# Two layers' first tiles multiplied before their norm, the last norm on turned rows, and another dealing of modulation work over the first block

## The reference

```
def second_block(x, c, ...):
    for l in range(DEPTH_2):
        x = decoder_layer(x, c, ...)
    return rms_norm_2(x, final_norm_g)

def decoder_layer(x, c, ...):
    mod = jax.nn.silu(c.astype(F32)) @ w_ada + b_ada
    shift1, scale1, gate1, shift2, scale2, gate2 = jnp.split(mod, 6, axis=-1)
    h = modulate(rms_norm_2(x, norm1_g), shift1, scale1)
    p = h @ w_in
    ...
    x = x + (gate1[:, None, :] * (merged.astype(x.dtype) @ w_o)).astype(x.dtype)
    h2 = modulate(rms_norm_2(x, norm2_g), shift2, scale2)
    y_moe = hier_moe(h2, ...)
    x = x + (gate2[:, None, :] * y_moe).astype(x.dtype)

def rms_norm_2(x, g):
    y = xf * lax.rsqrt(jnp.mean(xf * xf, axis=-1, keepdims=True) + NORM_EPS)
    return (y * g.astype(F32)).astype(x.dtype)
def modulate(h, shift, scale):
    return (h.astype(F32) * (1.0 + scale[:, None, :]) + shift[:, None, :]).astype(h.dtype)
```

## Time and profile before

| | us |
|---|---|
| median of 3 runs | 1968.52 (1965.6 to 1969.34) |
| profiled execution, its own time | 1964.88 |
| span of the profiled execution | 1963.1 |
| barrier between first block and layer 0 | 314.85 |

### The profile page before, as it was taken

How to read it: one execution, slowest core, us unless ns; L and a number is a source line. 1 busy time by engine, 2 the same in 40 slices (tenths; PEclk the granted TensorE clock), 3 DMA queues, 4 the chain that set the end, 5 groups by cost and what they waited for, 6 DMA issues and landing times.

```text
span 1963.1 us, 24328 instructions
## 1 busy us (share of the span) xinstructions
PE 1630.3 (83%) x10843; PEld 1104.7 (56%) x10843; DVE 531.9 (27%) x1049; ACT 318.3 (16%) x630; POOL 17.5 (1%) x25
## 2 busy tenths in 40 slices
PE   7999899999999996665666599999999866665666
PEld 6776678887888852222222177878888322221223
DVE  4887972644111120000000037131022100000002
ACT  2432312322200020000000042221011100000001
POOL 0010000000000000000000000000000000000000
PEclk9999899999999998878888899999999988787888
DMA  7798954313359379999999952134773999999996
GB/s 274 268 392 328 346 214 161 130 45 104 133 202 388 137 317 429 431 433 427 434 429 431 422 195 87 45 129 172 285 293 150 406 429 434 428 431 433 429 429 284
DMA packets 90364, 585.72 MB, mean 298 GB/s; under 512 B 12248, under 2 KB 15120, under 8 KB 69648
## 3 DMA queue, kind: packets, MB, share of 16 engines
q1 hardware_dynamic: 87664, 580.30, 72.8%
q10 hardware_dynamic: 2592, 3.81, 0.6%
HBM read 583.01 MB, written 1.08 MB: 298 GB/s over the span
## 4 chain that ended last, share of the span: by engine, by line
PE 47%; DMA 33%; DVE 3%; ACT 1%; issue 0%; SPq 0%
DMA expert_halves<-in_w_exp_down 18%; PE ps L1335 13%; DMA expert_halves<-in_w_exp_up 11%; PE ps L2215 8%; PE ps L2576 8%; DMA expert_halves<-in_w_exp_gate 4%; PE ps L2228 4%; PE ps L2253 3%; PE ps L2596 1%; PE ps L1338 1%; PE ps L2562 1%; PE ps L1585 1%; PE ps L1832 0%; DVE base_products L2000 0%; DVE gram L1955 0%; PE ps L1842 0%
## 5 line engine op out<-in xcount | busy, mean ns | idle before, releaser
L2576 PE MATMUL ps<-expert_halves,gathered 128*32 128x512 f32 x2048 | 308.0, 759 | 201.1 <-DMA expert_halves<-in_w_exp_up 125.2
L2576 PEld LDWEIGHTS ps<-expert_halves,gathered 128*32 128x32 f32 x2048 | 74.9, 134 | 424.3 <-issue 193.2
L1335 PE MATMUL ps<-h,ring 128*128 128x256 f32 x1216 | 274.4, 382 | 0.0
L1335 PEld LDWEIGHTS ps<-h,ring 128*128 128x128 f32 x1216 | 227.8, 190 | 37.0 <-issue 4.5
L2712 DVE TENSOR_TENSOR gate_up_rows<-gate_up_rows,ps 128x512 f32<-128x512 f32 x16 | 11.0, 688 | 735.9 <-PE ps L2576 735.9
L2576 PE MATMUL ps<-expert_halves,gate_up_turned 128*32 128x512 f32 x1024 | 144.4, 715 | 78.4 <-DMA expert_halves<-in_w_exp_down 70.5
L2215 PE MATMUL ps<-h,ring 128*128 128x256 f32 x768 | 166.7, 379 | 0.0
L2215 PEld LDWEIGHTS ps<-h,ring 128*128 128x128 f32 x768 | 145.9, 190 | 19.8
L268 PE MATMUL ps<-u,ring 128*128 128x256 f32 x640 | 146.3, 383 | 0.8 <-ACT xbc_raw L358 0.8
L2576 PEld LDWEIGHTS ps<-expert_halves,gate_up_turned 128*32 128x32 f32 x1024 | 34.9, 128 | 175.4 <-issue 84.2
L268 PEld LDWEIGHTS ps<-u,ring 128*128 128x128 f32 x640 | 119.5, 190 | 22.1 <-issue 4.2
(11 more groups left out here) (472 smaller groups left out, 1455.1 us busy)
## 6 DMA issues: line engine op xcount, KB each, us to landing
expert_halves<-in_w_exp_gate SPq DMA_DIRECT2D x30, 4096.0 KB, 43.1
expert_halves<-in_w_exp_up SPq DMA_DIRECT2D x30, 4096.0 KB, 43.1
expert_halves<-in_w_exp_down SPq DMA_DIRECT2D x26, 4096.0 KB, 43.3
ring<-in_w_in SPq DMA_DIRECT2D x31, 2048.0 KB, 9.0
ada_ring<-in_w_ada SPq DMA_DIRECT2D x48, 1024.0 KB, 7.3
ring<-in_w_gate SPq DMA_DIRECT2D x12, 2048.0 KB, 7.9
expert_halves<-in_w_exp_down SPq DMA_DIRECT2D x8, 2048.0 KB, 9.5
ring<-in_w_branch SPq DMA_DIRECT2D x6, 2048.0 KB, 7.6
```

The lines of the kernel that those rows point to most:

```text
L1335: ins = nc.tensor.matmul(k.ps[:, IN_BANK[t], 0:S], slab[:, j, c:c + w], k.h[:, j, :], start=j == 0, stop=j == ND - 1)
L2576: ins = nc.tensor.matmul(k.ps[r, bank, :], left[:, at + j, r], rows[:, i, :], start=at + j == 0, stop=last and j == 3)
```

## The change

**Dealing.** `ADA_BEHIND`, `ADA_AT`, the late places and the arguments of `scale` change. Pieces 0 to 2 stand behind slab 2 instead of slab 3 and wait for tile 0 instead of tile 7; six rows are done ahead of the last convolution, four before the scan loop (as before), one instead of two in each of its turns, up to 48 instead of 42 before the attention, and fewer in most of the attention's turns. **Early tiles.** In both layers the first two input tiles are multiplied with x times its gain (`gains`), with the shift as a 257th column; VectorE multiplies them by 1/rms afterwards and adds the shift column. The mean takes five matmuls instead of eight, since VectorE sums the first four squared tiles. Two slabs of layer 0 are asked for before the barrier, and one activation table is loaded before it. **End.** The sum over features is taken on turned rows, so that x is turned unscaled, as it becomes ready.

```diff
-ADA_BEHIND = (0, 0, 0, 3, 0, 3, 6, 5, 4, 5, 5, 5, 5, 5, 2)
+ADA_BEHIND = (0, 0, 3, 0, 0, 3, 2, 4, 7, 5, 4, 6, 4, 4, 6)
...
-ADA_AT = (19, 21, 23, 26, 30, 33, 36, 39, 41)
+ADA_AT = (18, 21, 23, 26, 29, 32, 36, 39, 41)
 ADA_STEPS = {t: [("sum", g)] for g, t in enumerate(ADA_AT)}
 ADA_STEPS |= {t + 1: [("turn", g)] for g, t in enumerate(ADA_AT)}
-LATE_STEPS = [[], [], [("sum", 9)], [("turn", 9)]] + 8 * [[]] + [[("sum", 10)], [("turn", 10)]] + 4 * [[]] + [[("sum", 11)], [("turn", 11)]] + 4 * [[]]
+LATE_AT = ((5, 6), (16, 19), (22, 23))
+LATE_STEPS = [[] for _ in range(3 * ND)]
+for _g, (_s, _t) in enumerate(LATE_AT):
+    LATE_STEPS[_s], LATE_STEPS[_t] = [("sum", len(ADA_AT) + _g)], [("turn", len(ADA_AT) + _g)]
 ada_steps = lambda t: ADA_STEPS[t] if t in ADA_STEPS else []
...
                 if p == 0:
-                    sp.wait_ge(sem.tile_done, 8)
+                    sp.wait_ge(sem.tile_done, 1)
...
+        for i in range(N_EARLY):
+            sp.wait_ge(sem.out_used, i + 2)
+            mix_load(k, sp, 0, i)
...
+        f.scale(dve, 6)
...
-        f.scale(dve, 4)
+        f.scale(dve, 10)
...
-            f.scale(dve, 4 + 2 * (r + 1))
+            f.scale(dve, 10 + r + 1)
...
-        f.scale(dve, 34)
+        f.scale(dve, 32)
...
-QK_AT = 42
+QK_AT = 48
...
-            f.scale(dve, 52 + (j + 1) * 5)
+            f.scale(dve, (56, 60, 64, 68, 76, 80)[j])
...
+        nc.scalar.preload_act_table_set("natural_log_exp_and_others")
...
-        f.scale(dve, 86)
+        f.scale(dve, 84)
...
-        f.scale(dve, 91)
+        f.scale(dve, 88)
...
+N_EARLY = 2
...
+            if t < N_EARLY:
+                if t == 0:
+                    pe.wait_ge(self.sem.gx_ready, self.past.gx_ready + j + 1)
+                ins = nc.tensor.matmul(k.ps[:, IN_BANK[t], 0:S + 1], slab[:, j, c:c + w], k.gx[:, j, 0:S + 1],
+                                       start=j == 0, stop=j == ND - 1)
+                if j == ND - 1:
+                    ins.then_inc(self.sem.tile_done, 1)
+                self.made += 1
+                continue
...
+        y.products(pe, 4)
         mean_of_squares(k, y, pe)
+        y.products(pe, N_EARLY * ND)
         if y.l == 0:
             router_products(k, y, pe)
-        else:
-            keep_busy(k, pe, 1, 9)
...
+            gains(k, y, dve, range(ND))
+            sum_four(k, y, dve)
             router_weights(k, y, dve)
+        else:
+            gains(k, y, dve, range(4, ND))
...
+        for t in range(N_EARLY):
+            dve.wait_ge(sem.tile_done, past.tile_done + t + 1)
+            nc.vector.tensor_tensor(k.early[:, t, :], k.ps[:, IN_BANK[t], 0:S], k.rstd[:, :], ALU.mult)
+            nc.vector.tensor_copy(k.early_shift[:, t:t + 1], k.ps[:, IN_BANK[t], S:S + 1]).then_inc(sem.normed, 1)
+            dve.wait_ge(sem.normed, past.normed + 2 * t + 3)
+            nc.vector.tensor_scalar(k.early[:, t, :], k.early[:, t, :], k.early_shift[:, t:t + 1], None, ALU.add
+                                    ).then_inc(sem.normed, 1)
...
+def sum_four(k, y, dve):
+
+
+    sem, past = y.sem, y.past
+    two = lambda a: k.h[:, a:a + 2, :]
+    dve.wait_ge(sem.squared, past.squared + 2)
+    dve.tensor_tensor(two(0), two(0), two(2), ALU.add).then_inc(sem.normed, 1)
+    dve.wait_ge(sem.normed, past.normed + 1)
+    dve.tensor_tensor(k.h[:, 0, :], k.h[:, 0, :], k.h[:, 1, :], ALU.add).then_inc(sem.normed, 1)
+
+
+def gains(k, y, dve, tiles):
+
+
+    mod = k.mod[:, y.l, :]
+    for j in tiles:
+        if j == 0:
+            dve.tensor_copy(k.gx[:, :, S], mod[:, 0:ND])
+        dve.tensor_scalar(k.gx[:, j, 0:S], k.x[:, j, :], mod[:, ND + j:ND + j + 1], None, ALU.mult).then_inc(y.sem.gx_ready, 1)
 
 
 def mean_of_squares(k, y, pe):
     sem, past = y.sem, y.past
-    for j in range(ND):
-        if j % 2 == 0:
-            pe.wait_ge(sem.squared, past.squared + j // 2 + 1)
-        ins = pe.matmul(k.ps[:, 2, 0:S], k.const("mean_d"), k.h[:, j, :], start=j == 0, stop=j == ND - 1)
+    pe.wait_ge(sem.normed, past.normed + 2)
+    for n, j in enumerate((0, 4, 5, 6, 7)):
+        if n % 2 == 1:
+            pe.wait_ge(sem.squared, past.squared + 3 + n // 2)
+        ins = pe.matmul(k.ps[:, 2, 0:S], k.const("mean_d"), k.h[:, j, :], start=n == 0, stop=n == 4)
...
+            if j == 3 and y.l < LAYERS - 1:
+                dve.wait_ge(sem.x_updated, past.x_updated + 4)
+                gains(k, y.next, dve, range(4))
+                sum_four(k, y.next, dve)
...
+            last = q == N_QUAD - 1 and l == LAYERS - 1
+            if last:
+                final_spread(k, y, pe)
...
+                if l == LAYERS - 1:
+                    for pair in range(2):
+                        final_turns(k, y, pe, pair)
...
+            if q == N_QUAD - 1 and y.l < LAYERS - 1:
+                for i in range(2):
+                    act.wait_ge(sem.x_updated, past.x_updated + 2 * i + 2)
+                    square_pair(k, y.next, act, i)
...
+def final_turns(k, y, pe, pair):
+
+    pe.wait_ge(y.sem.x_updated, y.past.x_updated + 2 * pair + 2)
+    for j in (2 * pair, 2 * pair + 1):
+        for t in range(NT):
+            ins = pe.transpose(k.ps[:, 2 + j // 4 * 2 + t, j % 4 * P:(j % 4 + 1) * P], k.x[:, j, t * P:(t + 1) * P], k.const("ident"))
+    ins.then_inc(y.sem.final_turned, 1)
...
+        for n, (b, t) in enumerate(((0, 0), (0, 1), (1, 0), (1, 1))):
+            act.wait_ge(sem.final_turned, 2 * b + 2)
+            if n == 3:
+                act.wait_ge(sem.final_scaled, 3)
+            nc.scalar.activation(k.final_junk[:, b, t, :], turned(b, t), ACT.Square, accum_out=k.final_sums[:, t, b:b + 1]
+                                 ).then_inc(sem.squared, 1)
+        act.wait_ge(sem.mean_done, past.mean_done + 2)
+        nc.scalar.activation(k.final_rstd[:, :], k.final_rstd[:, :], ACT.Ln, bias=k.eps[:, 0:1], scale=1.0 / D).then_inc(sem.ln_done, 1)
+        act.wait_ge(sem.ln_done, past.ln_done + 3)
+        nc.scalar.activation(k.final_rstd[:, :], k.final_rstd[:, :], ACT.Exp, scale=-0.5).then_inc(sem.rstd_done, 1)
...
+        for n, (b, t) in enumerate(((0, 0), (0, 1), (1, 1), (1, 0))):
+            dve.wait_ge(sem.final_turned, 2 * b + 2)
+            if n != 2:
+                dve.wait_ge(sem.squared, past.squared + ND // 2 + min(n, 2) + 1)
+            nc.vector.tensor_tensor(k.y_tok[:, t, cols(b)], turned(b, t), k.final_gain[:, cols(b)], ALU.mult
+                                    ).then_inc(sem.final_scaled, 1)
+        dve.wait_ge(sem.squared, past.squared + ND // 2 + 4)
+        nc.vector.tensor_reduce(k.final_rstd[:, :], k.final_sums[:, :, :], AX.X, ALU.add).then_inc(sem.mean_done, 1)
+        dve.wait_ge(sem.rstd_done, past.rstd_done + 3)
```

More of the change, by code:

```diff
@@ L1196, in first_block @@
     first_memory(k)
+    k.mix_loaded = [nc.alloc_semaphore(name=f"mix_slot{i}_loaded") for i in range(SLOTS)]
     one = [nc.alloc_semaphore(name=n) for n in FIRST_SIGNALS]
@@ L1443, in early @@
                 load_steps(3, 0, 2, sem.half_loaded[3][l])
-        for i in range(SLOTS):
+        for i in range(0 if l else N_EARLY, SLOTS):
             if l:
@@ L1595, in rwkv_inputs @@
     pair_ps = lambda b, j: k.ps[:, b + j // 2, j % 2 * S:j % 2 * S + S]
+    tile = lambda t: k.early[:, t, :] if t < N_EARLY else k.ps[:, IN_BANK[t], 0:S]
     flat = lambda t: t.rearrange("p j s -> p (j s)")
@@ L2836, in second_block @@
     memory_map(k)
-    k.mix_loaded = [nc.alloc_semaphore(name=f"mix_slot{i}_loaded") for i in range(SLOTS)]
     sems = Signals(*(nc.alloc_semaphore(name=n) for n in SIGNALS),
@@ L2845, in second_block @@
                     for l in range(LAYERS)])
+    layers = [Layer(k, l, sems) for l in range(LAYERS)]
+    for y, following in zip(layers, layers[1:]):
+        y.next = following
     with nc.Block() as block:
         for l in range(LAYERS):
-            y = Layer(k, l, sems)
+            y = layers[l]
             layer_loads(k, y, block)
@@ L2858, in second_block, with final_spread @@
             add_experts(k, y, block)
-        finish(k, Layer(k, LAYERS, sems), block)
+        finish(k, y, block)
+def final_spread(k, y, pe):
+    gain = k.cols_2[0]["final"]
+    for j in range(ND):
+        ins = pe.matmul(k.ps[:, 2 + j // 4, j % 4 * P:(j % 4 + 1) * P], gain[:, j:j + 1].broadcast_to([P, P]), k.const("ident"),
+                        start=True, stop=True)
+    ins.then_inc(y.sem.final_gain, 1)
+def final_turns(k, y, pe, pair):
[4 more added lines that the diff above has]
+    ins.then_inc(y.sem.final_turned, 1)
```

83 lines of the change are left out of this document (43 added, 40 removed).

## The result

The changed kernel takes 2018.1 us (median of 4 runs, 2014.1 to 2020.9), the kernel before 1968.9 in the same comparison: ratio 1.025, 95% interval 1.0236 to 1.0264. It is 49 us slower; the forecast was 32 slower, and the time lies 4 us above the upper end of the range. The profiled execution is the one of 2020.93 us.

A forecast was written before the change was run, and what follows sets the result against it. Bound: TensorE paces the first block; VectorE's rows wait for pieces behind slabs that wait for tiles. Sum: 36.6 + 7 - 2 - 5 - 4 = +32.6 on 1964.9, 1997.5, stated as 2000 by the median; range 1979 to 2014.

The forecast's parts named there:

- step 6: Attention: the two wide tiles cover most of the wait for pieces behind slab 10; 34.8 us behind at the output products.
- step 8: TensorE's low clock behind five new waits of 6 to 12 us: 1.4 us lost at each, 7 in all.
- steps 2 to 5: Scan loop to first logits: rows wait for pieces behind slabs that wait for TensorE's tiles; 34.6 us behind at the logits.
- step 1: Start of the scan loop: piece 3 lands at about 81.5; 2.9 us later, or 9.5 if SP is no earlier.
- (2): Third scan turn: row 12's piece stands behind slab 6; the fourth scan product starts at 104.9, 6.5 us after TensorE is ready.
- (3): Seventh scan turn: row 16's piece stands behind slab 7; the last scan product starts at 129.9, 15.9 us behind.
- (4): Sum behind tile 26: rows 24 to 31 need pieces behind slab 8 and end at 168.9; 25.1 us behind.
- (5): Sum behind tile 29 waits 9.3 us for rows 38 and 39; first logits at 205.4, 34.6 us behind.
- Step 7: Output: rows 84 to 95 stand behind slab 14, the last sum waits some 7 us; barrier at 351.4, 36.6 behind.
- Rival (b): Worse case: SP isn't earlier at the start (+6.5), low clock costs 3 us a wait (+8): 2005 to 2020, 17 in 100.
- The boundaries: Early tiles and the end: gains of 2 us in layer 0, 5 in layer 1 and 4 at the end.

The follow-up runs named there:

- the one-line kernel: The changed kernel with only the pieces put back behind their old slabs (`ADA_BEHIND`): 1962.3 us, ratio 0.9971 to the kernel before.
- e3: The changed kernel with idle matmuls on TensorE in front of six of its long waits: 2016.4 us, ratio 1.024 to the kernel before.
- e10: The changed kernel with one piece, number 8, moved from behind slab 7 to behind slab 6: 2011.5 us, ratio 1.0219 to the kernel before.
- e7: The changed kernel with ScalarE's copy of sum 10 put ahead of its square root: 2019.4 us, ratio 1.0262 to the kernel before.

## Why the prediction was right in kind and wrong in size

The time lies above the stated range, and the barrier, forecast between 348 and 365, stands at 377.50. Two steps failed: step 6 left out a wait for ScalarE, and step 8 booked too little for TensorE's low clock, at which steps 2 to 5 had not been walked. Each step's forecast beside what the trace after shows, with the miss that was added since the line above:

| place | forecast | after | miss added |
|---|---|---|---|
| first scan product (step 1: 86.82 + 2.9) | 89.7 | 92.72 | 3.0 |
| fourth scan product (2) | 104.9 | 110.38 | 2.5 |
| last scan product (3) | 129.9 | 137.88 | 2.5 |
| sum behind tile 26 (4) | 168.9 | 179.30 | 2.4 |
| sum behind tile 29 (5) | 189.8 | 202.35 | 2.2 |
| first logits (5) | 205.4 | 220.67 | 2.7 |
| output products (6: 246.75 + 34.8) | 281.6 | 307.05 | 10.2 |
| barrier (7: 314.9 + 36.6) | 351.5 | 377.50 | 0.5 |

*The mechanism was right.* All four stalls of steps 2 to 5 are where they were said to be, with waits of 6.1, 12.2, 11.7 and 9.4 for VectorE's rows (forecast 6.5, about 12, 11.4 and 9.3). That they come from the pieces behind the slabs is shown by the one-line kernel, and that they hang on each other by the one with piece 8.

*Step 6 failed*: "the two wide tiles (7.1 us each) cover most of it", "34.8 behind at the output products". The first wide tile covers 7 us, the second none if a turn stands between them that has to wait. The change moved sum 5 from tile 33 to 32, and with it the turn to tile 33, ahead of the second wide tile; that was in the table, and I walked only VectorE's rows through the attention, not ScalarE's list. ScalarE's copy of the sum stood there behind exponentials that waited for rows 48 to 51, and TensorE waited 9.5 for the copy. It is the largest single miss: 10.2 on the way to the output products, of which the kernel that moves the sum back recovers 7.9 (9.0 in the time). The place alone does no harm: the one-line kernel has its turn there too, with pieces 24 and 25 a slab earlier, and no turn of it waits over 2 us.

*Steps 2 to 5 walked TensorE at the full clock, and step 8 booked too little for it.* They missed 12.3 in sum. The stretches that TensorE runs right behind a wait, up to the slab's request or the logits, hold 11.8 of that. SP asks for slabs 8 and 9 in the change at:

```profile
158.53 0.38 SPq L390 DMA_DIRECT2D ring<-in_w_in  x1
...
189.53 0.38 SPq L390 DMA_DIRECT2D ring<-in_w_in  x1
```

| stretch of TensorE | forecast | after | with idle matmuls (e3) |
|---|---|---|---|
| first scan product to slab 6 | 2.0 | 4.0 | 2.2 |
| fourth scan product to slab 7 | 12.8 | 15.4 | 14.8 |
| last scan product to slab 8 | 18.3 | 20.7 | 19.8 |
| sum behind tile 26 to slab 9 | 8.1 | 10.2 | 8.2 |
| sum behind tile 29 to first logits | 15.6 | 18.3 | 15.9 |

In the first, fourth and fifth the idle matmuls kept the clock up, and there they come within 0.3 of the forecast. In the second and third the clock was low again even with them; but where the last scan product had hardly waited (e10), the next sum followed it in 4.2 us, against 6.5 in the change, so 2.2 of the third stretch's 2.4 are clock as well. For the second it is not shown how much is clock and how much TensorE's work that the walk left out. What lies between these stretches, slab, piece, rows, came out as walked: from slab 7 to the last scan product 12.1 (forecast 12.2), from slab 8 to its sum 20.8 (20.7), from slab 9 to its sum 12.8 (12.8).

So these five stretches lost 2.0 to 2.7 each, nearly all of it to the low clock, where I had taken 1.4 a wait; and none went free, since each ends in a request or in the logits that the next work waits for. (Step 8 counted only four of these waits; the one of 5.3 before the first scan product it left out.) What a full clock would give in the time is not shown. The kernels with idle matmuls got 1.1 and 1.4 at the barrier and 1.8 and 1.3 in the time, net of longer loads. The rule of the Trainium skill (TensorE: Matmul & The Clock Gate, Why this matters for your kernels), no idle gaps between bursts of matmuls, agrees with the trace at all five waits: the granted clock was 0.50 to 0.61 in the 4 to 7 us right behind them.

*Step 1* was 3.0 too short, mostly piece 3, 3.8 behind its slab instead of 2.5, and slab 5 asked at 70.5 instead of 68.7. Two executions with the same lists up to there differ by 1.6 at this point.

*Step 7* was 0.5 off, and the rows were as late as said. In the change the turn before the last sum waited 5.2 for ScalarE, which hid the wait for them; with that turn's wait gone (e7), the last sum waits 6.9 for the rows, forecast some 7. *The boundaries* were right: 2, 5 and 4 forecast, 2.5, 5.2 and 3.7 read. The kernel with the old dealing shows 9 us of them in the time, since the table load and the later rows take some back in the output.

Sum for the profiled execution: 26.0 beyond the forecast at the barrier, which are 3.0 at the start, 12.3 up to the logits, 10.2 in the attention and 0.5 in the output. Less the 7 booked for the clock that is 19.0; with 4.8 in the layers between and 0.4 less from the boundaries it is 23.4, from the +32.6 forecast to +56.0. By the medians the miss is 18. Rival (b) has the right range, 2005 to 2020, in part by luck: SP was earlier than before, by 4.9, where (b) had it no earlier; its 3 us of clock a wait were nearer than my 1.4. The rest was a wait that none of my cases named.
